# Moving the gating and splitting of two attention stages into their own loops, with the sigmoid gate taken from tanh

## What is computed

```python
# even mixer, for lat (512 rows) and ctx (256 rows)
aq, ak, av, ag, bq, bk, bv, bg = split_cols(h @ w_in, EVEN_WIDTHS)
...
y_lat = jnp.concatenate([oa * jax.nn.silu(ag), ob * jax.nn.silu(bg)], axis=-1) @ w_out
y_ctx = jnp.concatenate([oa_c * jax.nn.silu(c_ag), ob_c * jax.nn.silu(c_bg)], axis=-1) @ w_out
x_lat = x_lat + g_l[:, None, :] * y_lat
x_ctx = x_ctx + g_c * y_ctx
...
# odd mixer, lat only for the output
u = val * jax.nn.sigmoid(glu_gate)
u = conv31(u, dw_w) + dw_b
oc = jax.nn.silu(layer_norm(u, ln_g, ln_b)) * jax.nn.silu(silu_gate)      # silu_gate is cg
od = neighbourhood_attention(dq, dk, dv, rpb)
y_lat = jnp.concatenate([oc, od * jax.nn.silu(dg)], axis=-1) @ w_out
```

## Time and profile before

| what | us |
|---|---|
| median of 3 runs | 2920.94 |
| the profiled execution | 2919.86 |
| its span | 2918.1 |
| PE busy in it | 2662.5 (91%) |
| DVE busy | 1735.5 (59%) |
| ACT busy | 1103.5 (38%) |

### The profile page before, as it was taken

How to read it: one execution, slowest core, us unless ns; L and a number is a source line. 1 busy time by engine, 2 the same in 40 slices (tenths; PEclk the granted TensorE clock), 3 DMA queues, 4 the chain that set the end, 5 groups by cost and what they waited for, 6 DMA issues and landing times.

```text
span 2918.1 us, 35136 instructions
## 1 busy us (share of the span) xinstructions
PE 2662.5 (91%) x13456; PEld 2127.0 (73%) x13456; DVE 1735.5 (59%) x3382; ACT 1103.5 (38%) x1999; POOL 0.2 (0%) x4
## 2 busy tenths in 40 slices
PE   7997899989999899878999899998889997899888
PEld 5865878668888678668886688887766666787566
DVE  6657656454446775575554554476476674388653
ACT  4243244443322332432434433223336674322562
POOL 0000000000000000000000000000000000000000
PEclk9989999989999999899999899998999998799898
DMA  4210023123336423100331233364110000122311
GB/s 146 97 55 8 1 74 122 51 65 99 96 95 209 159 74 100 40 1 1 109 106 48 70 99 97 116 207 142 44 44 16 16 23 29 38 74 71 68 43 44
DMA packets 73365, 218.35 MB, mean 75 GB/s; under 512 B 21232, under 2 KB 21488, under 8 KB 72560
## 3 DMA queue, kind: packets, MB, share of 16 engines
q1 hardware_dynamic: 48384, 176.29, 19.0%
q10 hardware_dynamic: 24816, 39.82, 4.4%
HBM read 213.98 MB, written 2.10 MB: 74 GB/s over the span
## 4 chain that ended last, share of the span: by engine, by line
PE 74%; DVE 14%; ACT 5%; issue 4%; DMA 1%; ACTq 1%; DVEq 0%; SPq 0%
PE bank L574 18%; PE bank L575 18%; PE bank L576 18%; PE bank L765 4%; PE bank L729 3%; DVE mod_part L2362 3%; PE bank L739 3%; ACT w_hi L533 2%; PE bank L1185 2%; PE bank L1554 2%; PE bank L1199 1%; DVE w_lo L540 1%; PE bank L1194 1%; DVE hT L700 1%; PE bank L1129 1%
## 5 line engine op out<-in xcount | busy, mean ns | idle before, releaser
L574 PE MATMUL bank<-a_hi,w_hi 128*128 128x512 f32 (+1 forms) x1552 | 624.2, 402 | 43.7 <-ACT a_hi L603 21.7
L575 PE MATMUL bank<-a_lo,w_hi 128*128 128x512 f32 (+1 forms) x1552 | 613.2, 395 | 0.0
L576 PE MATMUL bank<-a_hi,w_lo 128*128 128x512 f32 (+1 forms) x1552 | 612.7, 395 | 0.0
L540 DVE TENSOR_TENSOR w_lo<-w_raw,w_hi 128x1024 fp32r<-128x1024 f32 x334 | 407.6, 1223 | 304.6 <-ACT w_hi L533 303.3
L533 ACT ACTIVATE w_hi<-w_raw 128x1024 fp32r<-128x1024 f32 x334 | 352.5, 1060 | 582.6 <-PE bank L576 488.7
L574 PEld LDWEIGHTS bank<-a_hi,w_hi 128*128 128x128 f32 (+1 forms) x1552 | 294.7, 190 | 131.7 <-issue 46.7
L576 PEld LDWEIGHTS bank<-a_hi,w_lo 128*128 128x128 f32 (+1 forms) x1552 | 295.2, 190 | 65.3
L575 PEld LDWEIGHTS bank<-a_lo,w_hi 128*128 128x128 f32 (+1 forms) x1552 | 295.7, 191 | 63.9 <-issue 2.7
L574 PE MATMUL bank<-b_hi,w_hi 128*128 128x512 f32 (+1 forms) x800 | 299.7, 375 | 36.4 <-DVE b_lo L713 23.5
L575 PE MATMUL bank<-b_lo,w_hi 128*128 128x512 f32 (+1 forms) x800 | 288.9, 361 | 0.0
L576 PE MATMUL bank<-b_hi,w_lo 128*128 128x512 f32 (+1 forms) x800 | 286.8, 358 | 0.0
(11 more groups left out here) (365 smaller groups left out, 3846.1 us busy)
## 6 DMA issues: line engine op xcount, KB each, us to landing
w_raw<-w_tiles SPq DMA_DIRECT2D x334, 512.0 KB, 3.4
mod_raw<-mod_tiles ACTq DMA_DIRECT2D x48, 512.0 KB, 3.5
d_bias<-rpb_rows ACTq DMA_DIRECT2D x16, 224.0 KB, 4.6
hT<-xT ACTq DMA_DIRECT2D x4, 512.0 KB, 11.1
m_in<-memT ACTq DMA_DIRECT2D x2, 1024.0 KB, 4.7
mod_cond<-cond_rows ACTq DMA_DIRECT2D x2, 1024.0 KB, 5.4
out<-hT ACTq DMA_DIRECT2D x8, 256.0 KB, 2.2
cT<-ctxT ACTq DMA_DIRECT2D x1, 1024.0 KB, 7.1
```

Of the source, the lines that this page charges most:

```text
L540: dve.tensor_tensor(w_lo[:, t % SPLIT, :], w_raw[:, t % RAW, :], w_hi[:, t % SPLIT, :].bitcast(f32), ALU.subtract).then_inc(sem("w_split"), 1)
L574: pe.matmul(o, wh, hi[:, k, :n], start=k == 0, stop=False)
L575: pe.matmul(o, wh, lo[:, k, :n], start=False, stop=False)
L576: mm = pe.matmul(o, wl, hi[:, k, :n], start=False, stop=k == kc - 1)
```

## The change

- The gate becomes tanh: silu(x) = 0.5 x (1 + tanh(x/2)). ACT writes tanh(x/2) of the bank to the gate's buffer, DVE makes (tanh + 1) * x with the bank as second operand, and so it is DVE, not ACT, that frees the gate's bank. The factor 0.5 is put into the multiply of the gating.
- Gating and splitting of a chunk move from behind the loop into it: `between` of the next chunk's steps. DVE gets per chunk: gate (L1845 of the changed kernel, twice 512/256 in the even stage), low part of a weight tile, gated multiply (L1867), and low part (L1871); ACT gets the rounding.
- The rounded part goes to the gate's own buffer and the low part to the buffer of the chunk itself (`twin` gives one place two types), so `b_hi` and `b_lo` stay in use for the gate products.
- Even filling: gate 0 is a plain product before the attention; gates 1 to 6 are filled in, 7 blocks per chunk, none in the last chunk; gate 7 is filled into the two turning steps behind the last scores, 4 blocks each.
- Odd filling: the transposes of d_v and gate cg0 are put before the sums of the convolution, gate dg0 after its variance; 5 gates are filled in at 2 or 3 blocks per step, and the last at 4 and 4 behind the last scores. The order of the odd gates becomes cg0, dg0, dg1, cg1, dg2, cg2, cg3, dg3.
- The squares of the second normalisation use `tmp`, since `sq` now shares its place with a gate buffer.

```diff
+    for name in ("cg0", "dg0", "dg1", "cg1", "dg2", "cg2", "cg3", "dg3"):
+        jobs.append((name, at[name[:2]] + P * int(name[2]), P, False))
...
+        EVEN_STEPS = KC * (TT + MT)
+        def even_gate_sum(i):
+            full, rest = divmod(min(i, EVEN_STEPS), TT + MT)
+            return min(7 * full + rest, KC * (KC - 2)) + KC // 2 * max(0, i - EVEN_STEPS)
         def even_gate_blocks(i):
-            return 1 if i % (TT + MT) < TT else 2
+            return even_gate_sum(i + 1) - even_gate_sum(i)
+        def even_gate_unit(c):
+            return 2 * next(i for i in range(2 * EVEN_STEPS) if even_gate_sum(i + 1) >= KC * c)
+        def even_gated_unit(c):
+            return max(2 * (TT + MT) * (c + 1) + 6, even_gate_unit(c) + 4)
...
+        def even_gate_act(act, c):
+            for p, _, sl, n, _ in PARTS:
+                b = bank(act, f"{E_GATE[c]}/{p}", 0)
+                act.activation(even_gate(c)[:, sl], b[:, :n], ACT.Tanh, scale=0.5).then_inc(*done("e_tanh", c, p))
+            hi_after(act, f"{E_GATE[c]}/lat", 0)
+        def even_gate_dve(dve, c):
+            for p, _, sl, n, _ in PARTS:
+                g = even_gate(c)[:, sl]
+                b = bank(dve, f"{E_GATE[c]}/{p}", 0)
+                dve.wait_ge(*when("e_tanh", c, p))
+                dve.scalar_tensor_tensor(out=g, in0=g, scalar=1.0, in1=b[:, :n], op0=ALU.add, op1=ALU.mult)\
+                   .then_inc(*freed(f"{E_GATE[c]}/{p}", 0, also=("e_gate", c, p)))
+            lo_after(dve, f"{E_GATE[c]}/lat", 0)
+        def even_between_act(act, u):
             for c in range(KC):
-                dve.wait_ge(*when("e_gate", c))
-                dve.tensor_tensor(e_q[:, c, :], e_q[:, c, :], even_gate(c), ALU.mult).then_inc(*done("e_gated", c))
+                if c and u == even_gate_unit(c):
+                    even_gate_act(act, c)
+                if u == even_gated_unit(c) + 2:
+                    act.wait_ge(*when("e_gated", c))
+                    act.activation(even_high(c), e_q[:, c, :], ACT.Copy).then_inc(*done("hi", "e_mix", c))
+        def even_between_dve(dve, u):
             for c in range(KC):
-                split_dve(dve, e_q[:, c, :], c, ("e_mix",), n=S + M, hi=b_hi, lo=b_lo)
+                if c and u == even_gate_unit(c):
+                    even_gate_dve(dve, c)
+                if u == even_gated_unit(c):
+                    for p in ("lat", "ctx"):
+                        dve.wait_ge(*when("e_gate", c, p))
+                    for third in range(3):
+                        dve.wait_ge(*when("e_out", c, third))
+                    x = e_q[:, c, :]
+                    dve.scalar_tensor_tensor(out=x, in0=x, scalar=0.5, in1=even_gate(c), op0=ALU.mult, op1=ALU.mult)\
+                       .then_inc(*done("e_gated", c))
+                if u == even_gated_unit(c) + 4:
+                    dve.wait_ge(*when("hi", "e_mix", c))
+                    dve.tensor_tensor(e_lo[:, c, :], e_q[:, c, :], even_high(c).bitcast(f32), ALU.subtract)\
+                       .then_inc(*done("lo", "e_mix", c))
...
+        def odd_gate_sum(i):
+            return (5 * min(i, ODD_STEPS) + 1) // 2 + KC // 2 * max(0, i - ODD_STEPS)
+        def odd_gate_unit(g):
+            return 2 * next(i for i in range(2 * ODD_STEPS) if odd_gate_sum(i + 1) >= KC * (g - 1))
+        def odd_gated_unit(g):
+            c = odd_chunk(ODD_GATE[g])
+            first = 4 if g < 2 else odd_gate_unit(g) + 4
+            return first if c < CC else max(first, 2 * TT * (c - CC + 1) + 6)
...
         def second_pe(pe):
             even_in_pe(pe)
+            product(pe, (0,), both(E_GATE[0]))
             attention_pe(pe, ("even",), even_units(), e_s, pair_tiles(e_pt), even_values,
...
             odd_in_pe(pe)
+            odd_turn_pe(pe)
+            product(pe, (1,), both(ODD_GATE[0])[:1])
             conformer_pe(pe)
-            odd_turn_pe(pe)
+            product(pe, (1,), both(ODD_GATE[1])[:1])
             attention_pe(pe, ("odd",), odd_units(), d_s, pair_tiles(d_pt),
-                         fill=odd_gate_steps(pe), blocks=lambda i: 4)
+                         fill=odd_gate_steps(pe), blocks=lambda i: odd_gate_sum(i + 1) - odd_gate_sum(i))
```

214 lines of the change are left out of this document (116 added, 98 removed).

## The result

The changed kernel took 2932.46 us (median of 6 runs, 2924.16 to 2933.29) beside 2919.38 us for the kernel before (6 runs, 2913.63 to 2922.34). The ratio is 1.0043, with a 95% interval of 1.0032 to 1.0054: slower by 13 us, where I had forecast 13.5 us less. Its profiled execution took 2933.26 us, with a span of 2931.4. All medians here are of fast executions; one of e6 (5956 us) and two of e8 (5246 and 5925 us) were slow and are left out.

A forecast was written before the change was run, and what follows sets the result against it. PE paces the even loop, with some 46 us of idle at the stages' ends. Even -7.0 + 4.5 and odd -13.0 + 2 sum to -13.5: 2907 us against 2920.94; forecast case 2898 to 2915, range 2888 to 2921.

The forecast's parts named there:

- C: Rival: each of 11 gate steps in the loops costs 5.8 us, gated multiplies uncovered too; near 2953 us; chance 0.08.
- my signs for being wrong: In the profile after: no gate-step stalls (Rival A), stalls at all eleven (C), or idle staying ahead of an output product.
- Start of the even stage: Gate 0's 8 blocks fill the 8.49 us idle ahead of the scores; DVE's work is about 1 over; net +0.3.
- Gate steps: Even loop: DVE's gate work delays the second unit's maxima, costing 1.6, 3.4, 3.3, 3.5 and 0; 11.8 us in all.
- Gated multiplies: Even loop: the gated multiply, beside a gate step or in a light step, adds some 2.0 us over seven chunks.
- The blocks that left: Even loop, chunks 0 to 6: 7 blocks per chunk instead of 8, 7 x 1.04 = -7.3 us.
- The last chunk: Even stage's end: six steps without blocks at DVE's pace, 22.4 plus 2.1 us; from step 41 to output product -13.8.
- Odd start: Transposes of d_v and cg0's blocks ahead of the sums move the first odd maxima by 8.2 us, to near 2726.9.
- Odd loop: Eight pairs of steps, six at the larger of two engines plus uncovered gate work: 103.9 us; odd stage -13.0.
- Odd tail: Last gate's blocks (5.5) and last values (2.8) fill 8 us of turning steps; output product starts near 2839.
- Clock: Mid-loop waits lower the clock: 1.5 us for each of three even stalls, 4.5, and 2 in the odd loop.
- Rival A: PE's pending banks and DVE's 84 us of slack cover the inserts: about 2878 us, half of it about 2892; chance 0.15.

The follow-up runs named there:

- e6: On top of e4, the gated multiply, its rounding and its low part also one unit later in the even loop; 2915.24 us, ratio 0.9990.
- e8: On top of e7, DVE's gate multiplies and low weight parts in the odd loop also one unit later; 2910.68 us, ratio 0.9972.
- e4: Changed kernel with DVE's even-loop gate work one unit later, behind both units' maxima of the step; 2920.24 us, ratio 1.0008.
- e9: Changed kernel with only the weight tile's low part behind both units' maxima in the even loop; 2923.67 us, ratio 1.0021.
- e3: Changed kernel with gate 7's 8 blocks in the last even chunk's steps and none in the turning steps; 2924.8 us, ratio 1.0019.
- e12: All repairs, e3, e6 and e8, in one kernel; 2897.32 us, ratio 0.9932.
- e5: On top of e2, ACT issues the bias tables and column mask ahead of the tanh of cg0 and dg0; 2921.71 us, ratio 1.0009.
- e11: Changed kernel with e5's edit alone, transposes and cg0 still ahead of the sums; 2927.38 us, ratio 1.0036.
- e7: The edits of e4 and e5 together; 2911.66 us, ratio 0.9975.
- e10: Changed kernel without DVE's gate multiplies of gates 1 to 6 in the even loop, ACT's tanh freeing the bank; 2930.67 us, ratio 1.0039.
- e1: Changed kernel with the odd stage's functions and order as before, only the even part changed; 2926.9 us, ratio 1.0031.
- e2: Changed kernel with d_v's transposes and gate cg0 put behind the convolution's variance again, odd sums first; 2929.66 us, ratio 1.0037.

## Why the prediction was wrong

The time lies outside the range and on the other side. No rival that I gave is what happened: C had every gate step stall at 5.8 us, and the stalls that came were mostly of the forecast's own size. Of my signs for being wrong C's came nearest: waits of 0.5 to 3.4 us stand at nearly all gate steps, not the 5.8 each of C. The steps that failed are four: the last even chunk at DVE's pace (5.6 us, with the tail behind it), the start of the odd stage (3.1), and, the largest, the odd loop (8) and the odd tail (6 to 7), where I let engines and steps overlap that wait for each other. In the order of the steps:

- **Start of the even stage.** Forecast +0.3, measured +1.0 by step 3. The size is off by little.
- **Gate steps.** Step 6 cost 1.4 (forecast 1.6), step 20 3.3 (3.3), step 27 3.2 (3.5). Step 14 cost 6.5 instead of 3.4, with a low clock in it, and step 28 1.1 more, with a low clock behind step 27's wait. The ctx gate of step 34 cost 0.7 where I had 0 (steps 35 and 36 took 4.41 and 5.16, and 3.81 and 5.01 in e4). The sum is 16.2, and 11.8 with the 4.5 set aside for the clock is 16.3: the walk through the banks was right in size and place, and the clock's share came out right in sum, by luck in part: it fell at two of the three stalls, and cost 3.3 and 1.1 and not 1.5 each.
- **Gated multiplies.** They took 0.9 in each of five light steps, 4.4 in all, where I had 2.0. e6 takes the 4.3 away.
- **The blocks that left.** Forecast 7 x 1.04 = 7.3. Steps 4 and 5, 10 and 11, 16 and 17, 22 and 23 are 0.95 shorter together, step 40 0.9. Steps 28 and 29 are only 0.3 shorter and 34 and 35 only 0.7, since they carry the 1.1 and 0.6 of the point above; in e9 and e4, without these, it is 1.3 and 1.3. In all 7.3: this term was right. The stretch to step 41 came out at +14.4 and not +11.3.
- **The last chunk (the failed step of the even stage).** I took its six steps at DVE's pace, 22.4 + 2.1, and PE at 20.35. Five of them took 31.0 us. Neither engine sets that time (PE busy 22.93 and DVE 22.27 of 31.0): without blocks PE waits in turn for DVE's maxima (1.0, 0.7, 1.3) and for ACT's copies (1.1, 1.7, 2.0), and the clock there is 0.83. From step 41 on the stage gained 8 us instead of 13.8. e3 shows it (26.05 with blocks back), and e12 shows it more clearly, with 12 us from step 42 on. The terms that I listed for this stretch add up to 43.1 and not to the 44.1 I used, and they have no place for step 41's own work (2.8) but for a stall of 2.3 in it that didn't come; these slips nearly cancel.
- **Odd start.** Forecast +8.2, measured +11.3. I listed ACT's loads as hanging on silu, and didn't ask what else the change put ahead of them in ACT's program and beside them in the queues: the issue train of 8.7 us became 13.0. e5 and e11 show the place of the loads to be the cause of 4 us.
- **Odd loop.** From the first maxima to the last divide I had 104 to 105 us, the trace has 112.6 (2738.06 to 2850.69; before 110.0). I let the larger of two engines set each pair of steps; PE was busy 99.3 and DVE 85.3 of 113. PE waits 3.1, 1.8, 2.1, 0.9 and 1.8 at steps 2, 7, 9, 10 and 12. The clock over the loop is 0.91, and 0.97 before. Moving the gate work by one unit takes 6 us of the loop away in e8's profile (105.9 beside e7's 112.1), and 3 of them come back in the tail.
- **Odd tail.** From the last divide to the output product I had 7 to 8 us, the trace has 14.3 (2850.69 to 2864.96). Two value products of 2.8, the transposes and the blocks keep PE busy 12.1 of 14.0 us behind that divide; I had counted one value product, and no transposes. This is read from the timeline; no run tests it.
- **Clock.** I forecast +6.5 in the loops, 4.5 even and 2 odd. At the even gate steps it is 3.3 in step 14 (6.5 less the wait of 3.17) and 1.1 in step 28. The last chunk's 0.83 I had not counted. In the odd loop 0.91 over 113 us and 0.97 over 110 before are 10.2 and 3.3 us, so the change cost at most 7 us there; this is an estimate, and too high where PE had nothing to do.

Windows of the odd loop and the odd tail, changed kernel, and the odd loop before and in e8:

```profile
2738.00:2851.00 113.00, 99.32 (x546) 66.05 (x547) 85.26 (x251) 65.56 (x141) 0.00 (x0) 0.91 0.17 40
2851.00:2865.00 14.00, 12.14 (x89) 8.79 (x88) 4.71 (x7) 6.33 (x14) 0.00 (x0) 1.00 0.13 39
...
2719.00:2829.00 110.00, 105.72 (x606) 73.60 (x606) 78.89 (x238) 67.49 (x142) 0.00 (x0) 0.97 0.20 51
...
2715.00:2821.00 106.00, 92.84 (x538) 61.41 (x539) 83.94 (x250) 65.23 (x140) 0.00 (x0) 0.95 0.18 41
```

The even misses are 3.1 up to step 41 and 5.6 behind it, together the 8.7 between -2.5 and +6.2. The odd ones are 3.1 at the start, 8 in the loop and 6 to 7 in the tail, less the 2 that I had added for the clock, for the 16.2 between -11.0 and +5.2. With 1.9 of drift ahead of the stages that is the 26.8 between -13.5 and +13.3.

Rival A's thought, that DVE has 84 us of slack, was the right one to test, but the slack isn't where the change puts its work. The multiplies' time on DVE didn't matter (e10), the low part's did, because it ends the chain (e9), and the place of both mattered by 10 to 12 us (e4, e7). The clock fell behind or in waits of 1.82 (e9, step 14), 3.17 (step 14) and 3.41 us (step 27), and behind 3.09 us (step 20) it stayed up in the changed kernel and fell in e1. So the rule of the Trainium skill ("TensorE: Matmul & The Clock Gate", section "A second HAM failure mode: psum-queue depth-cycling"), that short idles with banks cycled make the clock go up and down, holds here at some gate steps and not at others.

## What to carry to other kernels

When work is put into a loop on an engine that has slack, ask what that engine's next instruction is and who waits for it: behind the unit whose banks are awaited it was 10 to 12 us cheaper than ahead of it, at the same work. Filling is cover for a chain as well as work, so a step that is emptied can run at the length of its chain and not at the pace of its busiest engine, as the last even chunk did. And a load that is issued from an engine's program waits for everything the change puts ahead of it there (6.0 us in e2); put the issues first.

## What the runs showed of the hardware that I had not expected

The length of a wait doesn't tell whether the clock falls, and a fall can cost more than the wait. In the seven profiles with the gate work of the changed kernel (it, e1, e2, e3, e5, e10, e11) the clock fell in or just behind the wait of 3.17 us in step 14 and that of 3.4 in step 27, in all seven. At the 3.09 in step 20 it fell in three of them (e1, e3, e5) and not in the other four. In e9 it fell at the end of a wait of 1.82 in step 14, and not behind 1.73 in step 20 and 2.07 in step 27. In e4 and in e7 the two waits at steps 27 and 28 are the same (1.11 and 1.14, 1.12 and 1.15), and step 28 took 7.04 in the one and 9.96 in the other:

```profile
2334.00:2341.00 7.00, 6.41 (x45) 4.47 (x45) 4.78 (x16) 4.90 (x16) 0.00 (x0) 1.00 0.26 77
...
2330.00:2337.00 7.00, 6.06 (x22) 3.77 (x24) 4.76 (x16) 2.98 (x9) 0.00 (x0) 0.53 0.25 77
```

(e4, then e7.) In e6 and e12, with waits of 0.27 and 2.01 there, it took 10.86 and 9.43. What decides is left open; a repair can move a fall instead of removing it. Second, nine loads issued in a row, eight of 224 KB and one of 32 KB, took ACT's queue 8.3 to 8.7 us in seven kernels, and 11.9 to 13.2 in the seven where weight tiles of 512 KB were asked for at the same time.
